# Attention pipeline stretched by one pair of heads: head output two slots behind, probability transposes behind the query and key products

## What is computed

```python
q = (rms_norm(h @ w_q_a, q_latent_norm) @ w_q_b).reshape(B, S, N_HEADS, QK_DIM)
q_nope = q[..., :QK_NOPE_DIM]
q_pe = apply_rope(q[..., QK_NOPE_DIM:], cos[:, :, None, :], sin[:, :, None, :])
# per block of 128 queries, e = end of the block
sc = (einsum('bqhd,bkhd->bhqk', q_nope[:, s0:e], k_nope[:, :e])
      + einsum('bqhr,bkr->bhqk', q_pe[:, s0:e], k_pe[:, :e])) * ATTN_SCALE
p = softmax(where(mask, sc, -inf))
o = einsum('bhqk,bkhd->bqhd', p, v[:, :e])
return o.reshape(B, S, N_HEADS * V_DIM) @ w_o
```

## Time and profile before

| what | value |
| --- | --- |
| median of 3 runs | 1820.53 us (1820.5 to 1821.93) |
| the profiled execution: span | 1818.9 us |
| TensorE busy | 1774.5 us, 98% |
| VectorE busy | 1163.2 us, 64% |
| ScalarE busy | 921.5 us, 51% |
| GpSimd busy | 188.2 us, 10% |
| slots of the heads, TensorE | 853 to 978 us, output projection from 978 us |
| granted TensorE clock, mean | 0.994 |

### The profile page before, as it was taken

How to read it: one execution, slowest core, us unless ns; L and a number is a source line. 1 busy time by engine, 2 the same in 40 slices (tenths; PEclk the granted TensorE clock), 3 DMA queues, 4 the chain that set the end, 5 groups by cost and what they waited for, 6 DMA issues and landing times.

```text
span 1818.9 us, 29323 instructions
## 1 busy us (share of the span) xinstructions
PE 1774.5 (98%) x10300; PEld 1571.6 (86%) x10300; DVE 1163.2 (64%) x1427; ACT 921.5 (51%) x1195; POOL 188.2 (10%) x198
## 2 busy tenths in 40 slices
PE   6899999999999999999999999999999999999997
PEld 5788888888888888888888888888888888888886
DVE  7766666556666666668777776666655566666554
ACT  3565655333445454456776456556533344445442
POOL 5400000000000001124322430000000000000112
PEclk8999999999999999999999999999999999999998
DMA  4555556654555565544334556555655455556541
GB/s 180 172 196 189 184 188 230 201 177 153 192 187 190 190 231 192 178 150 134 122 127 139 195 175 197 192 188 190 229 198 181 150 188 192 186 192 225 194 162 46
DMA packets 83998, 326.64 MB, mean 180 GB/s; under 512 B 9456, under 2 KB 9712, under 8 KB 83952
## 3 DMA queue, kind: packets, MB, share of 16 engines
q1 hardware_dynamic: 83952, 326.04, 54.2%
HBM read 323.91 MB, written 2.10 MB: 179 GB/s over the span
## 4 chain that ended last, share of the span: by engine, by line
PE 90%; DVE 5%; ACT 3%; issue 2%; POOL 0%; DMA 0%; DVEq 0%; SPq 0%; ACTq 0%; POOLq 0%
PE ps L373 57%; PE ps L374 30%; ACT w_hi L689 1%; DVE win_v L1080 1%; ACT product L845 1%; PE ps L435 0%; DVE xg L1031 0%; DVE w_lo L1021 0%; DMA x<-xT 0%; PE ps L527 0%; DVE prob L1355 0%; PE ps L526 0%; PE ps L525 0%; DVE pooled L1090 0%; ACT prob L905 0%
## 5 line engine op out<-in xcount | busy, mean ns | idle before, releaser
L1021 DVE TENSOR_TENSOR w_lo<-raw,w_hi 128x1024 fp32r<-128x1024 f32 (+2 forms) x557 | 731.3, 1315 | 422.6 <-ACT w_hi L689 422.1
L373 PE MATMUL ps<-xg,w_hi 128*128 128x512 f32 x2880 | 999.4, 390 | 1.0 <-POOL w_lo L1502 1.0
L689 ACT ACTIVATE w_hi<-raw 128x1024 fp32r<-128x1024 f32 (+2 forms) x562 | 630.2, 1124 | 494.5 <-PE ps L374 494.5
L374 PE MATMUL ps<-xg,w_lo 128*128 128x256 f32 x2880 | 812.2, 282 | 0.0
L373 PEld LDWEIGHTS ps<-xg,w_hi 128*128 128x128 f32 x2880 | 540.4, 188 | 114.7 <-POOL w_lo L1502 1.4
L374 PEld LDWEIGHTS ps<-xg,w_lo 128*128 128x128 f32 x2880 | 544.3, 189 | 0.1
L373 PE MATMUL ps<-act,w_hi 128*128 128x512 f32 x1408 | 488.3, 390 | 0.0
L374 PE MATMUL ps<-act,w_lo 128*128 128x256 f32 x1408 | 397.1, 282 | 0.0
L373 PEld LDWEIGHTS ps<-act,w_hi 128*128 128x128 f32 x1408 | 264.2, 188 | 55.4
L374 PEld LDWEIGHTS ps<-act,w_lo 128*128 128x128 f32 x1408 | 266.1, 189 | 0.0
L1467 POOL TENSOR_TENSOR square<-x 128x256 f32 (+1 forms) x47 | 42.4, 903 | 1452.0 <-DVE x L1151 1452.0
(11 more groups left out here) (168 smaller groups left out, 1202.5 us busy)
## 6 DMA issues: line engine op xcount, KB each, us to landing
raw<-w_gate SPq DMA_DIRECT2D x176, 512.0 KB, 3.5
raw<-w_up SPq DMA_DIRECT2D x176, 512.0 KB, 3.3
raw<-w_down SPq DMA_DIRECT2D x128, 704.0 KB, 4.1
raw<-w_o SPq DMA_DIRECT2D x32, 512.0 KB, 3.3
raw<-pool_w SPq DMA_DIRECT2D x8, 512.0 KB, 11.0
raw<-w_q_a SPq DMA_DIRECT2D x8, 512.0 KB, 3.3
raw<-w_kv_a SPq DMA_DIRECT2D x8, 512.0 KB, 3.3
raw<-w_q_nope SPq DMA_DIRECT2D x8, 512.0 KB, 3.3
```

The source lines that it names most:

```text
L373: pe.matmul(ps[:, bank, :], w_hi[:, s, j * P:(j + 1) * P], moving, start=start, stop=False)
L374: return pe.matmul(ps[:, bank, 0:SEQ], w_lo[:, s, j * P:(j + 1) * P], moving[:, 0:SEQ], start=False, stop=stop)
L689: nc.scalar.activation(dst, src, ACT.Copy).then_inc(hi_ready, 1)
L1021: nc.vector.tensor_tensor(lo, src, hi.bitcast(F32), ALU.subtract).then_inc(lo_ready, 1)
```

## The change

No product is added or left out. The order of the work is changed on three engines, from pair g on:

- TensorE: head output is one slot later (g-2 in slot g) and stands behind the query rope and ahead of the scores. The values are cut in two halves, and the transposes of g-1 stand between them. Behind the last slot the output projection is cut up in the same manner, with its chunks 4 and 5 each left open for the last two heads.
- ScalarE: the head copies stand ahead of the exponentials, the two pairs of exponentials come without the query's `cross` between them, which follows with `pair_hi`; the transposed probabilities are copied behind two splits, ahead of the values.
- VectorE: next split and head low halves stand ahead of the row maxima; the normalisation is done head by head and ahead of the query sum; the probabilities' low half stands behind two splits, ahead of the values' low half.

GpSimd and SyncE are as before.

```diff
-            def value_part(g, i=None):
+            def value_part(g, m, i=None):
...
-                pe.wait_ge(lo_ready, plus(made(n), i, BODY))
-                for m in range(2):
-                    bank_free(t + m, i, 16)
...
+                if m == 0:
+                    pe.wait_ge(lo_ready, plus(made(n), i, BODY))
+                bank_free(t + m, i, 16)
...
+                if m == 1:
+                    mm.then_inc(chunks_used, 1)
...
-            def wo_part(c, i=None, each=None):
+            def wo_part(c, i=None, js=range(TILES)):
...
             def slot(g, i=None):
...
+                query_rope_part(g, i)
+                if g >= 2:
+                    head_output(g - 2, 0, i)
+                    head_output(g - 2, 1, i)
                 if g >= 1:
                     scores(g - 1, 0, i)
                     scores(g - 1, 1, i)
...
+                query_part(g, i)
+                if g == 0:
+                    pe.wait_ge(lat_ready, 2 * LT)
+                key_part(g, i)
+                value_part(g, 0, i)
                 if g >= 1:
                     turn_probs(g - 1, 0, i)
                     turn_probs(g - 1, 1, i)
...
+                value_part(g, 1, i)
...
+            last = HG - 1
+            wo_part(0)
+            head_output(last - 1, 0)
+            head_output(last - 1, 1)
+            scores(last, 0)
+            scores(last, 1)
+            wo_part(1)
+            wo_part(2)
+            wo_part(3, js=range(TILES // 2))
+            turn_probs(last, 0)
+            turn_probs(last, 1)
+            wo_part(3, js=range(TILES // 2, TILES))
+            pe.wait_ge(head_split, last)
+            wo_part(4, js=range(TILES - 2))
+            head_output(last, 0)
+            head_output(last, 1)
+            wo_part(5, js=range(TILES - 2))
+            pe.wait_ge(head_split, HG)
+            wo_part(4, js=range(TILES - 2, TILES))
+            wo_part(5, js=range(TILES - 2, TILES))
+            for c in range(6, BODY):
                 wo_part(c)
...
@@ scalar, slot
+                    sc.wait_ge(evacuated, plus(TILE["heads"] + 8 * g + 2, i, 16))
+                    swap_halves(gate_act)
                     if g >= 2:
                         heads_hi_half(g - 2, i)
-                    probT_hi_half(g - 1, i)
+                    exps(g - 1, 0, i)
+                    exps(g - 1, 1, i)
+                    pair_cross(g, 1, i)
+                    pair_hi(g, 1, q_buf, i)
...
                 split(n + 2 + SPLIT_SLOTS, i)
+                if g >= 1:
+                    probT_hi_half(g - 1, i)
                 value_hi(g, i)
...
@@ vector
-            def normalise(g, i):
+            def normalise(g, hh, i):
...
+                ve.wait_ge(exp_ready, plus(4 * g + 2 * hh + 2, i, 8))
+                step(nc.vector.reciprocal(stat[:, hh, 6:8], stat[:, hh, 4:6]))
...
                     rope_add(g, cr + 1, i)
-                    row_max(g - 1, 0, i)
-                    row_max(g - 1, 1, i)
-                    pair_add(g, 1, cr + 2, i)
-                    normalise(g - 1, i)
                     split(n + SPLIT_SLOTS, i)
                     if g >= 2:
                         heads_lo_half(g - 2, i)
-                    probT_lo_half(g - 1, i)
+                    row_max(g - 1, 0, i)
+                    row_max(g - 1, 1, i)
+                    normalise(g - 1, 0, i)
+                    normalise(g - 1, 1, i)
+                    pair_add(g, 1, cr + 2, i)
                 pair_add(g, 2, cr + 3, i)
                 rope_lo(g, i)
                 split(n + 1 + SPLIT_SLOTS, i)
                 split(n + 2 + SPLIT_SLOTS, i)
+                if g >= 1:
+                    probT_lo_half(g - 1, i)
                 value_lo(g, i)
                 split(n + 3 + SPLIT_SLOTS, i)
```

More of the change, by code:

```diff
@@ L603, in wo_part @@
                 pe.wait_ge(lo_ready, plus(made(n), i, BODY))
-                if half == 0:
+                if half == 0 and js[0] == 0:
                     bank_free(t, i, 4)
-                for j in range(TILES):
+                for j in js:
                     kt = half * TILES + j
-                    if each is not None:
-                        each(kt)
                     mm = product3(n, j, t % 4, heads[:, kt, :], kt == 0, kt == DT - 1)
-                mm.then_inc(chunks_used, 1)
+                if js[-1] == TILES - 1:
+                    mm.then_inc(chunks_used, 1)
             def slot(g, i=None):
[L616 to L620, removed]
+                query_rope_part(g, i)
+                if g >= 2:
+                    head_output(g - 2, 0, i)
+                    head_output(g - 2, 1, i)
                 if g >= 1:
@@ L649, in _ @@
                 slot(3, i)
-            slot(HG)
-            wo_part(4, each=lambda kt: pe.wait_ge(head_split, kt // 2 + 1))
-            for c in range(5, BODY):
+            last = HG - 1
[19 more added lines that the diff above has]
+            for c in range(6, BODY):
                 wo_part(c)
@@ L922, in slot @@
                     key_hi_halves()
+                    sc.wait_ge(evacuated, TILE["heads"] + 2)
+                    swap_halves(gate_act)
+                    split(n + SPLIT_SLOTS)
                 else:
                     split(n + SPLIT_SLOTS, i)
[L926 to L934, removed]
+                    sc.wait_ge(evacuated, plus(TILE["heads"] + 8 * g + 2, i, 16))
+                    swap_halves(gate_act)
                     if g >= 2:
                         heads_hi_half(g - 2, i)
-                    probT_hi_half(g - 1, i)
+                    exps(g - 1, 0, i)
+                    exps(g - 1, 1, i)
+                    pair_cross(g, 1, i)
+                    pair_hi(g, 1, q_buf, i)
                 pair_cross(g, 2, i)
@@ L1348, in row_max @@
                 nc.vector.tensor_scalar(stat[:, hh, 2:4], stat[:, hh, 0:2], -1.0, None, ALU.mult).then_inc(max_ready, 1)
-            def normalise(g, i):
[L1352 to L1358, removed]
+            def normalise(g, hh, i):
+                ve.wait_ge(exp_ready, plus(4 * g + 2 * hh + 2, i, 8))
+                step(nc.vector.reciprocal(stat[:, hh, 6:8], stat[:, hh, 4:6]))
+                nc.vector.tensor_scalar(prob[:, hh, 0:P], prob[:, hh, 0:P], stat[:, hh, 6:7], None,
+                                        ALU.mult).then_inc(prob_ready, 1)
+                nc.vector.tensor_scalar(prob[:, hh, P:], prob[:, hh, P:], stat[:, hh, 7:8], None,
+                                        ALU.mult).then_inc(prob_ready, 1)
             lat_norm(KV, 1, G_LKV, beside=(key_add, key_scale))
@@ L1390, in _ @@
             slot(1)
-            loop(HG // 2 - 2, 2 * 4, lambda i: (slot(2, i), slot(3, i)))
+            loop(HG // 2 - 2, 2 * 5, lambda i: (slot(2, i), slot(3, i)))
             slot(HG - 2)
@@ L1398, in _ @@
             split(n1 + SPLIT_SLOTS)
+            heads_lo_half(HG - 2, None)
             row_max(HG - 1, 0, None)
             row_max(HG - 1, 1, None)
-            normalise(HG - 1, None)
-            heads_lo_half(HG - 2, None)
+            normalise(HG - 1, 0, None)
+            normalise(HG - 1, 1, None)
             split(n1 + 1 + SPLIT_SLOTS)
```

29 lines of the change are left out of this document (10 added, 19 removed).

## The result

The changed kernel takes 1842.78 us (median of 4 runs, 1840.85 to 1844.97) against 1820.74 for the kernel before: ratio 1.0118, 95% interval 1.0106 to 1.013. It is 22 us slower. 11.7 had been forecast: the sign and the account of the ring hold, the size doesn't, and the time lies 1.8 us above the range. The profiled execution is the shortest run, 1840.85 us with a span of 1839.1.

A forecast was written before the change was run, and what follows sets the result against it. The loop of ScalarE, VectorE and GpSimd was taken to bound the kernel. A later slot 1, six slots of 17.60 us and the tail gave +11.7: 1820.5 + 11.7 = 1832.2 us, range 1825 to 1841.

The forecast's parts named there:

- the ring: ScalarE, VectorE and GpSimd pass work round from weight splits through softmax and key sum; said to set the 15.8 us slot.
- The bound: TensorE is 98% busy with 7.4 us of waits at transposes; the other three engines' loop sets the 15.8 us slot.
- Where the new wait is: TensorE's stall moves from the transposes to head output, waiting for VectorE's probT: 3.0 us per slot instead of 1.14.
- The length of the ring: From one slot's first wide weight split on ScalarE to the next: 17.60 us, in six slots.
- terms of the head copies: Head copies now ahead of the softmax, in series: 0.64 us on ScalarE, then 1.00 on VectorE, with row_max queued behind.
- GpSimd's leg: Query's pair_hi to GpSimd 0.71 us, subtraction there 1.27; the key sum waits for it, so it is newly on the path.
- The port beside row_max: Row_max's first one-column copy might be held by GpSimd's rotation, 0.64 us per slot, 3.8 in all; zero was taken.
- The step that failed: the clock: Behind each 3.0 us TensorE stall 1.1 us of work lost, about absorbed by the scores' slack; 0.6 per slot allowed.
- only the wait moves: Rival: values wait for pair_add instead of the transposes, nothing else changes; 1820 us, chance 0.05.
- the kernel gets faster: Rival: probT is ready when TensorE arrives, the stall goes, about 9 us less; 1811.5 us, chance 0.05.
- The shorter ring through TensorE: Rival: key sum needn't wait for GpSimd, so the loop closes from head output to key end, 16.3 us; 1826, chance 0.07.
- Port and clock on top: Rival: row_max's copy held by GpSimd and a lowered TensorE clock add to the forecast; 1836 to 1841 us, chance 0.13.

The follow-up runs named there:

- experiment 6: Kernel before with one TensorE move each: values halved around the transposes, 1820.45 us; head output one slot later, 1821.47 us.
- 7: Kernel before with normalisation by head alone, 1821.3 us; with the first head's also put ahead of the query sum, 1813.45 us.
- experiment 5: Changed kernel with head copies back behind the softmax and query sum back ahead of normalisation, four filling products ahead of head output: 1844.51 us.
- experiment 4: Changed kernel with query sum back ahead of normalisation and cross copy between exponentials: 1836.96 us; with six filling products, 1827.33 us.
- experiment 2: Changed kernel with the head copies put back behind softmax and query sum, no filling: median 1831.82 us, from 1827.08 to 1844.5.
- experiments 1: Changed kernel with ten unread float32 products ahead of each head output and four in the tail: 1833.18 us.
- 3: Changed kernel with head copies back behind softmax and query sum, plus five filling products ahead of each head output: 1827.58 us.
- second run of 5: Changed kernel with head copies and query sum both put back, nine filling products instead of four ahead of head output: 1832.09 us.
- second part of experiment 6: Kernel before with only the head output moved, to pair g-2 behind the query rope, with the changed kernel's TensorE tail: 1821.47 us.

## Why the prediction failed, and what of it held

- **The bound.** Held. TensorE's idle time was small change, and the ring of the other three engines set the slot: moving TensorE's stall (experiment 6) gained nothing, shortening the ring (7) took the slot to TensorE's 14.6 us.
- **Where the new wait is.** Held: at L595 (L594 before the change), on probT of VectorE, six times and once more behind the last slot; next to none at the transposes; the key sum waits for GpSimd. The forecast 3.0 us came as 2.72, 2.95 and 2.89 where the slot before had run at full clock; behind a slot with the clock down the wait was 1.8 to 1.9.
- **The length of the ring.** 17.60 forecast. With the clock held 17.8 measured on average (106.75 us in six slots, forecast 105.6), and the whole kernel at 1833.2 where 1832.2 was forecast. The terms of the head copies and of GpSimd's leg were summed in series, and put back one by one they give 1.0 and 0.8 us. But they don't add up: with both back the slot was 17.8 again (experiment 5), by its rows because another path closes it, through the query products.
- **The port beside row_max.** The value taken, zero, was right: the copy ran at 0.15 us beside GpSimd. The upper value of 0.64 per slot was never used.
- **The step that failed: the clock.** The step said that 1.1 us of work is lost behind a wait of 3.0 us, that the scores have 1.1 to spare, and that this is about absorbed. Both halves of it were wrong. The 1.1 came from one window of 4 us that ended while the clock was still down; in the next 4 us it was 0.84, which makes 1.7 us for the two:

```profile
40.00:44.00 4.00, 4.00 (x17) 3.42 (x16) 3.90 (x4) 0.57 (x2) 3.84 (x3) 0.84 0.00 0
```

In the changed kernel it stayed down for 7 us, 3.4 us of work. And the scores were the wrong place to look: they came 2.4 us late and held VectorE for 0.49, but the slowed query products ended behind the exponentials and held the query's `cross` copy for 1.5 to 1.9 us in each of these slots. So the ring shut through TensorE: 19.8 us instead of 17.6. In the profiled run that is 6.7 us in three slots and 1.6 at the scores in the tail (4.38 instead of 2.77 us), together 8.3 of the 8.65 by which it exceeds the forecast. The other runs, 1841.84 to 1844.97 at mean clocks of 0.984 to 0.981 against 0.988, seem to have had more of it. The mechanism had been named among the unknown costs and the rivals, at 0.6 us per slot; it costs 2.2 in each slot in which it strikes.
- **The rivals.** That only the wait moves, or that the kernel gets faster, is refuted. The shorter ring through TensorE (16.3) was never reached: without GpSimd's leg 16.8 to 17.2 was measured with the clock held (experiment 4), with the ring still closed over the other engines, through the held scaling of 1.35 us. "Port and clock on top" (1836 to 1841) had the right sign but the port gave nothing and the clock more than its 4 us.

## What to carry to other kernels

Before stretching a pipeline to cover a stall of the busiest engine, follow the ring of the helpers once round and see which of the moved steps lie on it: in this case each of the two moves on TensorE was free by itself, and the copies put ahead of the softmax and the sum put behind it cost 1.0 and 0.8 us per slot. Such prices hold one at a time: with both paid back, another path held the slot at 17.8 us. Price a recurring idle time of TensorE with the clock, over all of the stretch in which the granted clock is below 1, and follow everything that TensorE does in that stretch to the step that waits for it, not only the first piece. And look for a single instruction that is four times its usual length: the cure here was a few lines that moved one scaling out of GpSimd's way, and two others into a wait.

## What the runs showed of the hardware

- The granted clock fell behind recurring waits as short as 1.8 to 2.1 us (in slots 3 to 7 of the profiled run of experiment 2). In the profiled runs with filling whose longest idle times ahead of the head output were 0.7 to 1.1 us, once 1.6, it didn't (experiments 1, 3 and 4, and the second run of 5). The length of one wait doesn't decide it: in the changed kernel the clock held behind 2.72 and 1.92 us and fell behind 1.28, and in the profiled run of the second part of experiment 6 it fell behind two waits of 0.79 and 0.95 us that stood 1.5 us apart. Runs of one and the same kernel differ by 17 us, and the mean clock goes with it. The Trainium skill, "TensorE: Matmul & The Clock Gate", Part 1, says that the gate's watch over TensorE's activity runs freely and isn't reset when a kernel starts, and that the point at which the clock changes varies for this reason; the scatter from 1827.08 to 1844.5 us is in line with it, but no run here isolates it.
- Idle work can pay: some 2.4 us of products that nobody reads in each of six slots, and four products behind the last, made the changed kernel 9.6 us faster.
- A one-column copy on VectorE was not held by GpSimd (0.15 us, inside a step of GpSimd), while a scaling of two columns was: its usual 0.17 us became 0.47 in slot 1 of the changed kernel (at 873.77, inside a step of GpSimd that had started at 873.47).
